# Hybrid attention block on one core: the conditioning row summed by VectorE, all of its remainders there, and the next block's first weights rounded inside the last gate tile

## What is computed

```python
ada = jax.nn.silu(c) @ w_ada[layer] + b_ada[layer]
shift, scale, gate = jnp.split(ada, 3, axis=-1)
h = _rms_norm(x, norm_g[layer]) * (1.0 + scale[:, None, :]) + shift[:, None, :]
proj = h @ w_in[layer]
(qa, ka, va, fa, za, qb, kb, vb, zb, ga, gb) = jnp.split(proj, offsets, axis=-1)
...
merged = jax.nn.sigmoid(ga) * ya + jax.nn.sigmoid(gb) * yb
x = x + gate[:, None, :] * (merged @ w_out[layer])
```

## Time and profile before

| | |
|---|---|
| median of 3 runs | 2040.95 us (2038.14 to 2043.18) |
| the profiled execution's own time | 2040.65 us |
| its span in the profile | 2038.8 us |
| busy: TensorE, VectorE, ScalarE, GpSimd | 1926.0, 918.2, 727.6, 547.8 us |
| mean granted clock of TensorE | 0.979 |
| the last gate tile's last matmul starts | 178.32 us |
| the next block's first matmul starts | 185.42 us |

### The profile page before, as it was taken

The page is one execution under the profiler, slowest core; times in us unless marked ns, Lnnn a source line. Parts: engine busy times, 40 slices in busy tenths (PEclk is TensorE's granted clock), DMA queues, the critical chain, the costliest instruction groups (busy, mean ns, idle before and its releaser), DMA issues. The chain is left out here.

```text
span 2038.8 us, 27725 instructions
## 1 busy us (share of the span) xinstructions
PE 1926.0 (94%) x9722; PEld 1544.3 (76%) x9722; DVE 918.2 (45%) x1931; ACT 727.6 (36%) x1335; POOL 547.8 (27%) x502
## 2 busy tenths in 40 slices
PE   7698999999999999999997889999999989999998
PEld 2577878788887887888885666667766669998887
DVE  1652565646522122210225556767676456555333
ACT  1561222222201122321204567787778770012100
POOL 1431000000000000000003567777778752110000
PEclk9699999999999999999998899999999999999999
DMA  7322243434444122121416256466646334233321
GB/s 248 114 83 96 83 125 93 123 93 144 145 103 129 47 93 82 50 88 46 142 42 144 53 119 159 106 143 149 135 108 140 103 116 135 83 103 122 105 104 72
DMA packets 236591, 222.69 MB, mean 109 GB/s; under 512 B 54738, under 2 KB 188626, under 8 KB 236468
## 3 DMA queue, kind: packets, MB, share of 16 engines
q1 hardware_dynamic: 223044, 180.95, 32.4%
q0 software_dynamic: 11648, 39.85, 6.1%
q10 hardware_dynamic: 1792, 0.53, 0.1%
HBM read 149.18 MB, written 71.70 MB: 108 GB/s over the span
## 5 line engine op out<-in xcount | busy, mean ns | idle before, releaser
L1361 POOL TENSOR_TENSOR Pl<-PT,Ph 128x512 fp32r<-128x512 f32 (+2 forms) x350 | 417.0, 1216 | 155.6 <-ACT Ph L1461 125.3
L546 PE MATMUL pj<-Wh,hTh 128*128 128x512 f32 (+1 forms) x640 | 244.6, 382 | 11.7 <-DVEq L735 6.7
L450 POOL DMA_DIRECT2D wraw<-in_w_in x72 | 38.6, 536 | 794.6 <-DVE Wl L750 760.1
L546 PE MATMUL pj<-hTh,Wh 128*128 128x512 f32 x640 | 249.7, 390 | 0.6 <-DVE Wl L750 0.3
L547 PE MATMUL pj<-hTl,Wh 128*128 128x512 f32 x640 | 249.1, 389 | 0.0
L548 PE MATMUL pj<-hTh,Wl 128*128 128x512 f32 x640 | 249.1, 389 | 0.0
L548 PE MATMUL pj<-Wh,hTl 128*128 128x512 f32 (+1 forms) x640 | 238.9, 373 | 0.0
L547 PE MATMUL pj<-Wl,hTh 128*128 128x512 f32 (+1 forms) x640 | 238.6, 373 | 0.0
L1454 ACT ACTIVATE PT<-sc 128x512 f32<-128x512 f32 (+2 forms) x350 | 191.7, 548 | 129.0 <-PE sc L1388 34.8
L1149 DVE TENSOR_REDUCE part_max<-mx 128x1 f32<-128x512 f32 (+3 forms) x267 | 159.4, 600 | 119.6 <-PE mx L1106 117.5
L1461 ACT ACTIVATE Ph<-PT 128x512 fp32r<-128x512 f32 (+2 forms) x350 | 207.9, 594 | 11.1
(11 more groups left out here) (263 smaller groups left out, 3711.1 us busy)
## 6 DMA issues: line engine op xcount, KB each, us to landing
qk_scratch<-qThl SPq DMA_DIRECT2D x96, 256.0 KB, 2.7
wraw<-in_w_in POOLq DMA_DIRECT2D x84, 256.0 KB, 4.0
g_scratch<-st SPq DMA_DIRECT2D x64, 256.0 KB, 2.4
gt<-g_scratch SPq DMA_DIRECT2D x16, 1024.0 KB, 7.8
xin<-in_x POOLq DMA_DIRECT2D x16, 512.0 KB, 5.0
wada<-in_w_ada SPq DMA_DIRECT2D x16, 512.0 KB, 6.5
z_scratch<-st SPq DMA_DIRECT2D x32, 256.0 KB, 2.4
Qb<-qk_scratch SPq DMA_DIRECT2D x32, 256.0 KB
```

The costliest lines, as they stand in the source:

```text
L546: nc.tensor.matmul(out, a_hi, b_hi, start=first, stop=False)
L1361: pool.tensor_tensor(Pl[n % NPH][0:rows, 0:w], PT[n % NP][0:rows, 0:w], Ph[n % NPH][0:rows, 0:w].bitcast(F32), ALU.subtract).then_inc(low_ ...
```

## The change

- VectorE sums the conditioning row: for each piece k it multiplies the piece by the column `siluc[:, k]` and adds it to `ada_sum` (in the buffer hf[1]), 128 partitions x 2048, in two halves (L340). TensorE then makes the 16 columns by products of ada_sum with a column of ones, which sums over the partitions (L245). The row products and the two copies go.
- The flips of pair 0 stand behind the first half of piece 6, those of pair 1 go to the banks of the gate tiles and wait for `cols_read` alone.
- The remainder of a pair is one VectorE operation of eight pieces (L387). GpSimd computes nothing in the block any more, and its loads wait for their buffers alone.
- From pair 2 on, `stats` and `inverse` of pair b + 1 precede hf of pair b on VectorE, and the two `root` on ScalarE.
- The weights' casts and remainders of the first four pieces stand ahead of `ab_ready`, the other four behind hf of pair 1. Tile 0 stands behind pair 1, tile 1 behind pair 2.
- The next block's casts stand ahead of the sigmoid of the last tile. The wait for the last stores is now the first thing on SP in `project`.

```diff
-    KA, KD = 6, 3
...
+    KA = 6
...
-    tiles_behind = {b: (2 * b - 4, 2 * b - 3) for b in range(2, NPAIR)}
+    tiles_behind = {1: (0,), 2: (1,)}
+    tiles_behind.update({b: (2 * b - 4, 2 * b - 3) for b in range(3, NPAIR)})
...
-        ada_row = ps_g.rearrange("p k n -> p (k n)")[0:1, :]
+        ps_pair1 = ps_g.rearrange("p k n -> p (k n)").rearrange("p (k n) -> p k n", n=PAIR)
...
+        ada_sum = hf[1].rearrange("p k n -> p (k n)")
+        one = sb("one_p", [P, 1])
...
+        def pair_banks(b):
+            return ps_pair1 if b == 1 else ps_x
...
-                    sp.wait_ge(ada_mm, k - WR + 1)
+                    sp.wait_ge(ada_added, 2 * (k - WR + 1))
...
-            for k in range(ST):
-                sp.wait_ge(gate_stored[k], 16 * TT // ST)
...
-            pool.wait_ge(ada_mm, KT - 3)
+            pool.wait_ge(ada_added, 2 * (KT - 3))
...
             load(XR)
             load(XR + 1)
             for b in range(NPAIR):
-                pool.wait_ge(hi_done, b + 1)
-                tok = slice(b * PAIR, (b + 1) * PAIR)
-                nc.gpsimd.tensor_tensor(hTl[:, KD:KT, tok], hf[b % 2][:, KD:KT, :], hTh[:, KD:KT, tok].bitcast(F32),
-                                        ALU.subtract).then_inc(lo_done, 1)
...
-                if b and t % 2 == 0:
-                    pe.wait_ge(full_act, KA * b)
-                    pe.wait_ge(full_dve, (KT - KA) * b)
+                if b == 1 and t % 2 == 0:
+                    pe.wait_ge(cols_read, 1)
+                if b >= 2 and t % 2 == 0:
+                    pe.wait_ge(full_act, KA * (b if b > 2 else 1))
+                    pe.wait_ge(full_dve, (KT - KA) * (b if b > 2 else 1))
                 for k in range(KT):
-                    mm = nc.tensor.transpose(ps_x[:, k, t % 2 * P:(t % 2 + 1) * P],
+                    mm = nc.tensor.transpose(pair_banks(b)[:, k, t % 2 * P:(t % 2 + 1) * P],
...
-                    for done in (hi_done, lo_done, lo_dve):
-                        pe.wait_ge(done, 2 * b + 2)
+                    pe.wait_ge(lo_done, 2 * b + 2)
...
-            pe.wait_ge(siluc_done, 1)
-            for k in range(KT):
-                pe.wait_ge(wada_in[k % WR], 32 * (k // WR + 1))
-                for n in range(0, 2 * D, 512):
-                    mm = nc.tensor.matmul(ada_row[:, n:n + 512], keep["siluc"][:, k:k + 1], wada[k % WR][n // D][:, n % D:n % D + 512],
-                                          start=k == 0, stop=k == KT - 1)
-                mm.then_inc(ada_mm, 1)
-                if k == KT // 2:
-                    pe.wait_ge(id_done, 2)
-                    flip(0)
-                    flip(1)
-            pe.wait_ge(row_act, 1)
-            pe.wait_ge(row_dve, 2)
+            pe.wait_ge(id_done, 2)
+            pe.wait_ge(ada_added, 2 * KT - 3)
+            flip(0)
+            flip(1)
+            pe.wait_ge(one_done, 1)
             for m in range(NADA):
-                mm = nc.tensor.matmul(ada_cols[:, m:m + 1], row[m // KT][:, m % KT * P:(m % KT + 1) * P], one[:], start=True, stop=True)
+                pe.wait_ge(ada_added, 2 * KT - 1 + m // KT)
+                mm = nc.tensor.matmul(ada_cols[:, m:m + 1], ada_sum[:, m * P:(m + 1) * P], one[:], start=True, stop=True)
             mm.then_inc(cols_done, 1)
-            pe.wait_ge(cols_read, 1)
...
-                if t + 1 < TT:
-                    root(t + 1)
...
-            root(0)
-            for t in range(XR - 2):
+            for t in range(0, XR, 2):
+                root(t)
+                root(t + 1)
                 normalise(t)
-            act.wait_ge(ada_mm, KT)
-            nc.scalar.activation(row[0], ada_row[:, 0:D], ACT.Copy).then_inc(row_act, 1)
-            normalise(XR - 2)
+                normalise(t + 1)
+            for k in range(RAW):
+                high(k)
             act.wait_ge(ab_ready, 1)
...
+                if 1 < b < NPAIR - 1:
+                    root(2 * b + 2)
+                    root(2 * b + 3)
...
-                    act.wait_ge(lo_dve, b - 1)
...
-                for t in (XR - 1 + 2 * b, XR + 2 * b):
-                    if t < TT:
-                        normalise(t)
-                if b < 2:
-                    for k in range(b * RAW, (b + 1) * RAW):
+                t = 2 * b + 2
+                if b == 1:
+                    for k in range(RAW, KT):
                         high(k)
+                    root(t)
+                    root(t + 1)
+                if 0 < b < NPAIR - 1:
+                    normalise(t)
+                    normalise(t + 1)
                 for n in tiles_behind.get(b, ()):
-                    gate(n)
+                    if n < TT - 1:
+                        gate(n)
             for k in range(KT):
                 if k < RAW:
                     act.wait_ge(w_in[k], 16 * (KT // RAW + 1))
@@ -317,6 +313,7 @@
                 else:
                     act.wait_ge(gate_mm, TT)
                 nc.scalar.activation(Wh[:, k, :], (wraw[k] if k < RAW else wlate[k - RAW])[:], ACT.Copy).then_inc(w_hi, 1)
+            gate(TT - 1)
...
-            def step(t):
-                if t < TT:
-                    stats(t)
-                if t <= TT:
-                    inverse(t - 1)
+            def ada_row(k):
+                dve.wait_ge(wada_in[k % WR], 32 * (k // WR + 1))
+                for half in range(2):
+                    total, factor = ada_sum[:, half * D:(half + 1) * D], keep["siluc"][:, k:k + 1]
+                    if k == 0:
+                        nc.vector.tensor_scalar(total, wada[0][half][:], factor, None, ALU.mult).then_inc(ada_added, 1)
+                    else:
+                        dve.wait_ge(ada_added, 2 * k - 1 + half)
+                        nc.vector.scalar_tensor_tensor(total, wada[k % WR][half][:], factor, total, ALU.mult, ALU.add
+                                                       ).then_inc(ada_added, 1)
...
+            nc.vector.memset(one[:], 1.0).then_inc(one_done, 1)
             stats(0)
-            for t in range(1, XR):
-                step(t)
-            nc.vector.memset(one[:], 1.0).then_inc(row_dve, 1)
-            dve.wait_ge(ada_mm, KT)
-            nc.vector.tensor_copy(row[1], ada_row[:, D:2 * D]).then_inc(row_dve, 1)
+            stats(1)
+            dve.wait_ge(siluc_done, 1)
+            ada_row(0)
+            inverse(0)
+            inverse(1)
+            for k in range(1, KT - 2):
+                ada_row(k)
+            stats(2)
+            ada_row(KT - 2)
+            stats(3)
+            ada_row(KT - 1)
+            inverse(2)
+            inverse(3)
+            for k in range(RAW):
+                low(0, k, wraw[k])
...
-                tok = slice(b * PAIR, (b + 1) * PAIR)
+                tok, t = slice(b * PAIR, (b + 1) * PAIR), 2 * b + 2
+                if 1 < b < NPAIR - 1:
+                    stats(t)
+                    stats(t + 1)
+                    inverse(t)
+                    inverse(t + 1)
...
-                nc.vector.tensor_tensor(hTl[:, 0:KD, tok], hf[b % 2][:, 0:KD, :], hTh[:, 0:KD, tok].bitcast(F32),
-                                        ALU.subtract).then_inc(lo_dve, 1)
-                step(XR + 2 * b)
-                step(XR + 2 * b + 1)
-                if b < 2:
-                    for k in range(b * RAW, (b + 1) * RAW):
+                nc.vector.tensor_tensor(hTl[:, :, tok], hf[b % 2][:], hTh[:, :, tok].bitcast(F32),
+                                        ALU.subtract).then_inc(lo_done, 1)
+                if b == 1:
+                    for k in range(RAW, KT):
                         low(0, k, wraw[k % RAW])
+                    stats(t)
+                    stats(t + 1)
+                    inverse(t)
+                    inverse(t + 1)
...
+            for done in keep["gate_stored"]:
+                sp.wait_ge(done, 16 * TT // 2)
```

16 lines of the change are left out of this document (7 added, 9 removed).

## The result

| | median us | runs |
|---|---|---|
| before | 2040.64 (2038.14 to 2043.18) | 4 |
| changed | 2009.43 (2005.37 to 2011.08) | 4 |

The ratio is 0.9834 [0.9816, 0.9852], the 95% interval in brackets. The profiled execution took 2011.08 us, span 2009.4, mean granted clock 0.985, where before took 2040.65, 2038.8 and 0.979. A second measurement of the same kernel, beside other runs of before: 2011.24 against 2042.33, 0.9858 [0.9838, 0.9878].

A forecast was written before the change was run, and what follows sets the result against it. It took the opening block's chain, from conditioning vector to first gate tile to next block's first matmul, as the bound. Gate tiles -21.5, join -4.3 and clock -2.6 make -28.4 from 2040.65: 2012 us, range 2005 to 2024.

The forecast's parts named there:

- multiply-add: Conditioning row on VectorE: each 128x1024 instruction takes 1.20 us, the pace of the squares.
- DMA behind the hole: After the 16 to 18 us spell with almost no DMA, which goes, transfers continue at 362 GB/s.
- sum ready: End of the conditioning row: VectorE has summed all pieces at 39.4 us.
- column products: TensorE's sixteen column products after the row start at 38.2 and take 5.4 us again.
- hf of pair 0: ScalarE and VectorE can start the first pair's hf at 45.4 us instead of 51.91.
- first gate tile: TensorE starts its first gate tile at 56.4 us instead of 77.69.
- gap at the join: TensorE's idle time before the next block falls from 6.7 to 2.4 us, saving 4.3.
- slow matmuls behind it: After the join the clock stays high, so 13 matmuls save 0.2 us each, 2.6 in all.
- Rival 1: Conditioning row: the instruction runs at the scan's pace, 2.4 us, VectorE bounds the row, total 2023.5 us; chance 0.12.
- late small loads: Next block's small loads start 2 to 3 us later relative to TensorE but stay hidden, by 1.7 us.
- rival 2: Join: the clock falls (+2.6 us) and later small loads stop TensorE after three tiles, total 2017 us; chance 0.09.
- Rival 3: Conditioning row: GpSimd's DMA issues or incoming data slow VectorE to 3.90 us an instruction, total 2044.4 us; chance 0.03.

The follow-up runs named there:

- join_undone: Changed kernel with the last sigmoid put ahead of the eight casts again; median 2018.53 us, ratio 0.9888.
- pool_back: Changed kernel with five of eight pieces of each remainder on GpSimd again; median 2017.32 us, ratio 0.9862.
- pool_noise: Changed kernel with two extra, unused GpSimd subtractions while VectorE sums the conditioning row; 2012.94 us, one run.
- warm_both: Changed kernel with 14 unused transposes at the join, 44 ahead of tile 0, and tiles 0 and 1 both behind pair 1; 2009.09 us, ratio 0.9839.
- join_alone: Kernel before with only the last sigmoid behind the casts and SP's store wait moved into the next block; 2038.79 us, ratio 0.9974.

## Why the prediction was right, point by point

Predicted 2012, measured 2009.43; 28.4 us against 29.6 between the two profiled executions. The mechanism held term by term, but so close an agreement is partly luck: hf came 2.9 us earlier than predicted, the clock behind the join gave back 1.8 less, and the two misses have opposite signs. The unchanged stages alone scatter by 9 us between profiled executions.

| step | predicted | measured in the profile |
|---|---|---|
| multiply-add | 1.20 | 1.24 |
| DMA behind the hole | 362 GB/s | 393 from 18 to 34 |
| sum ready | 39.4 | 36.63 (36.8 to 40.5 in variants) |
| column products | 5.4 | 4.58 (3.70 to 6.96) |
| hf of pair 0 | 45.4 | 42.50 (42.6 to 47.0) |
| first gate tile | 56.4 | 53.55 |
| start of hf to end of gate tiles | 111.8 | 111.43 |
| gap at the join | 2.4 | 2.35 |
| slow matmuls behind it | none, -2.6 | eight, -0.8 |

**The multiply-add** was the forecast's largest risk, and the row of squares was the right neighbour, the scan's the wrong one. Two instructions of 128x1024 with both tensors in SBUF as f32 take 2.48 us, as fast per instruction as the squares (1.22) or a plain subtraction of that size (1.22 in the kernel before). The rule cited against the change says that this form "halves throughput" (the Trainium skill, Vector Engine (DVE) Microarchitecture Reference, section 7, Points that are easy to get wrong). Read as the prediction read it, as twice the time of the squares, it is not what this case shows. The section does not say against what the half is meant; beside instructions that read one tensor the multiply-add is indeed slower, 1.24 against 0.71 for the multiplication of the same size and 1.23 for a cast of twice as many columns. Rival 1 falls either way.

**The conditioning row.** Here the mis-sized term is the DMA rate, which was underrated: DMA kept 393 GB/s from 18 to 34, the last half of w_ada landed at 33.96 and VectorE took it up at 34.15, so the sum was ready 2.8 us before the prediction's time. No row shows the 0.8 us that the prediction put between last byte and consumer; at piece 0 it is 0.1 (landed 11.05, taken up 11.15). Why the kernel before brought only 362 is not shown: windows of 2 us there reach 416 as well, but others stay at 315 to 350. Who is late next was right in the changed kernel: VectorE's queue with its four weight remainders, not the column products. In join_undone, pool_back, pool_noise and warm_both, with products of 6.96, the products ended last by 0.6. Part of the 2.9 us by which hf was early is scatter: piece 0 of w_ada is in at 11.15 in the changed kernel and by 11.4 in four of the variants, where hf starts at 42.6 to 44.3; in four others it is in at 12.3 to 12.6 and hf starts at 44.5 to 47.0.

**The pairs and the first tile** held to 0.4 us, and the runs divide that term: of 19.7 us between hf and the next block, the remainder on VectorE gives 5.0 alone and 3.8 in the new order, tile 0 behind pair 1 gives 6.4, the join 4.1 to 4.4. Some 4 to 5 are left for pair 1's own banks, the earlier weights and the earlier statistics, which were not tried one by one.

**The join.** The gap was right, and the late small loads are hidden: `wf` came 9.4 after the restart, not 10.8, and TensorE did not wait for them. The term that was mis-sized here is the clock: "With a gap of 2.4 I expect it to stay, which saves 13 times 0.2". In this execution it did not stay: eight slow matmuls instead of twelve (the prediction counted 13), which saves 0.8. In five of seven executions with this gap it did, and join_alone has the full 6.9. So the forecast described the commoner outcome and the profile shows the other; this half of rival 2 happens in part of the executions.

**Rival 3** did not happen. pool_noise shows that GpSimd's computing would hold a multiply-add for 2.6 to 3.3 us, under the 3.6 from which it would have decided; its DMA issues and the incoming data, which the rival named, leave it at 1.27.

## What to carry to other kernels

Price an instruction that is not in the trace by the row with the same operands and the same number of elements, and take another operation's pace as the far bound. When GpSimd shares a step with VectorE, count both its hold on VectorE's instructions and the DMA issues that stand ahead of it in its own queue; in pool_back the second was the larger. Before paying for a warm TensorE, look whether the engines that feed it have slack: here 1.6 us won at tile 0 came back as waits for ScalarE within two pairs.
